# Row sums of the second block's mixer from a 65th column of the values that holds 1.0

## The reference, cut to what matters

```python
def hybrid_mixer(n, pos, ...):
    proj = n @ w_in          # c_q 256, c_kv 128, k_r 32, dq, dk, dv 384 each, mq, mk, mv 256 each
    o_a = mla_causal_attention(q_a, k_a, v_a)            # 6 heads, keys 64 + 32, values 64
    o_b = diff_causal_attention(q1, q2, k1, k2, dv, ...) # 6 heads, p = softmax(s1) - lam * softmax(s2)
    o_b = rmsnorm(o_b, sub_norm) * (1.0 - lam_init)
    o_c = moba_causal_attention(mq, mk, mv, ...)         # 4 heads of 64; at 256 tokens one block
    return concatenate([o_a, o_b, o_c]) @ w_out
```

## Time and profile before

| what | value |
|---|---|
| runs | 2402.16, 2405.36, 2407.83 us, median 2405.36 |
| profiled execution | 2401.76 us, its span 2400.0 us |
| TensorE, matmuls | 2357.4 us busy, 98% of the span |
| TensorE, weight loads | 1937.0 us, 81% |
| VectorE | 1726.6 us, 72% |
| ScalarE | 1446.9 us, 60% |
| GpSimd | 69.7 us, 3% |
| TensorE's granted clock | 0.998 of full speed |
| first layer's mixer of the second stack | attention from about 1575.6 to 1635 us |
| the same of the second layer | about 2009.4 to 2069 us |

### The profile page before, as it was taken

One profiled execution on the slowest core, in us unless ns is written; L12 is line 12 of the kernel. 1 busy time (PEld: TensorE's weight loads), 2 busy tenths in 40 slices (PEclk: granted clock), 3 DMA queues, 4 the chain that ended last, 5 costly groups with the idle time before them and its releaser, 6 DMA issues.

```text
span 2400.0 us, 32057 instructions
## 1 busy us (share of the span) xinstructions
PE 2357.4 (98%) x12122; PEld 1937.0 (81%) x12122; DVE 1726.6 (72%) x2111; ACT 1446.9 (60%) x1761; POOL 69.7 (3%) x79
## 2 busy tenths in 40 slices
PE   9999999999999999999999999999999999999998
PEld 8688888678888888888888888888888888887887
DVE  8664446769898988888989898766465565755555
ACT  6544444657777777777777777564544446554443
POOL 1000000001000000000000000001000000000000
PEclk9999999999999999999999999999999999999999
DMA  7545554429999999999999999516435542452651
GB/s 264 163 158 193 185 186 157 145 82 340 368 345 372 344 377 345 374 339 375 348 369 346 369 350 366 192 54 227 159 124 192 177 145 83 175 187 95 196 190 44
DMA packets 249706, 569.99 MB, mean 237 GB/s; under 512 B 9665, under 2 KB 20353, under 8 KB 249601
## 3 DMA queue, kind: packets, MB, share of 16 engines
q1 hardware_dynamic: 249456, 568.30, 67.1%
q10 hardware_dynamic: 144, 0.26, 0.0%
HBM read 562.82 MB, written 1.05 MB: 235 GB/s over the span
## 4 chain that ended last, share of the span: by engine, by line
PE 92%; DVE 5%; ACT 2%; issue 1%; POOL 0%; POOLq 0%; ACTq 0%; DVEq 0%
PE PS L911 26%; PE PS L913 26%; PE PS L912 26%; PE PS L1064 2%; PE PS L1119 1%; PE PS L1534 1%; PE PS L1076 1%; PE PS L1363 1%; PE PS L1183 1%; PE PS L983 1%; ACT SM L1806 1%; DVE Wl L2216 1%; PE PS L1008 1%; PE PS L1102 1%; PE PS L1324 1%
## 5 line engine op out<-in xcount | busy, mean ns | idle before, releaser
L2645 DVE TENSOR_TENSOR Wl<-ring,Wh 128x2048 fp32r<-128x2048 f32 x334 | 761.6, 2297 | 101.0 <-ACT Wh L1952 101.0
L1952 ACT ACTIVATE Wh<-ring 128x2048 fp32r<-128x2048 f32 x334 | 639.8, 1918 | 127.7 <-PE PS L913 127.7
L2216 DVE TENSOR_TENSOR Wl<-ring,Wh 128x2048 fp32r<-128x2048 f32 (+2 forms) x192 | 431.0, 2251 | 276.6 <-ACT Wh L1713 276.1
L1713 ACT ACTIVATE Wh<-ring 128x2048 fp32r<-128x2048 f32 (+2 forms) x192 | 361.6, 1890 | 235.2 <-PE PS L913 234.2
L911 PE MATMUL PS<-Wh,HTh 128*128 128x512 f32 (+3 forms) x1184 | 464.2, 392 | 4.7 <-DVE Wl L2216 2.4
L913 PE MATMUL PS<-Wh,HTl 128*128 128x512 f32 (+3 forms) x1184 | 456.4, 386 | 0.0
L912 PE MATMUL PS<-Wl,HTh 128*128 128x512 f32 (+3 forms) x1184 | 455.4, 385 | 0.0
L911 PE MATMUL PS<-Wh,xgh 128*128 128x512 f32 x896 | 354.3, 395 | 1.8 <-DVE Wl L2645 1.2
L913 PE MATMUL PS<-Wh,xgl 128*128 128x512 f32 x896 | 349.5, 390 | 0.0
L912 PE MATMUL PS<-Wl,xgh 128*128 128x512 f32 x896 | 348.9, 389 | 0.0
L911 PEld LDWEIGHTS PS<-Wh,HTh 128*128 128x128 f32 x1184 | 222.8, 188 | 50.4 <-issue 4.3
(11 more groups left out here) (349 smaller groups left out, 2422.4 us busy)
## 6 DMA issues: line engine op xcount, KB each, us to landing
ring<-in_moe_w_gate SPq DMA_DIRECT2D x112, 1024.0 KB, 6.9
ring<-in_moe_w_up SPq DMA_DIRECT2D x112, 1024.0 KB, 7.0
ring<-in_moe_w_down SPq DMA_DIRECT2D x112, 1024.0 KB, 6.8
ring<-in_mlp_w SPq DMA_DIRECT2D x64, 1024.0 KB, 5.2
ring<-in_w_in SPq DMA_DIRECT2D x27, 1024.0 KB, 5.3
ring<-in_w_out SPq DMA_DIRECT2D x16, 1024.0 KB, 7.1
ring<-in_cross_wkv SPq DMA_DIRECT2D x16, 1024.0 KB, 12.4
ring<-in_ffn_w_gate SPq DMA_DIRECT2D x14, 1024.0 KB, 5.1
```

What stands on the lines that cost most here:

```text
L1713: act.activation(Wh[:, i % SPLITS, 0:n], ring[:, r % RING, 0:n], ACT.Copy).then_inc(w_hi, 1)
L1952: act.activation(Wh[:, (base + i) % SPLITS, :], ring[:, (raw + i) % RING, :], ACT.Copy).then_inc(e_hi, 1)
L2216: dve.tensor_tensor(Wl[:, i % SPLITS, 0:n], ring[:, r % RING, 0:n], Wh[:, i % SPLITS, 0:n].bitcast(F32), ALU.subtract).then_inc(w_lo, 1)
L2645: dve.tensor_tensor(Wl[:, (base + i) % SPLITS, :], ring[:, (raw + i) % RING, :], Wh[:, (base + i) % SPLITS, :].bitcast(F32), ALU.subtract) ...
```

## The change

The value tiles of diff (`DVS`), moba (`MVS`) and MLA (`VV`) get 65 columns per head. VectorE writes 1.0 into the last of them, six small memsets a layer. The value products read 65 columns per head, so that the output has the row's sum behind its 64 numbers, and `end` takes the reciprocal from there, in PSUM. The exponentials lose the accumulator output, and the wait for the output four units back that protected `sums`. To lay the values out with gaps, `take_block` (blocks 2 and 3) and `take_last` use two copies where there was one. The columns of `proj` behind the diff values move: moba's q starts at 1574 (before: 1568), its k at 1830, its v at 2086. `proj` has 2352 columns instead of 2336 for each of two tiles, 128 bytes more. Cross attention and the first stack stay as they are.

```diff
--- before.py
+++ after.py
@@ -96,6 +96,12 @@
 C1W = 28 + CC * TAPS
 C2 = dict(attn=0, cross=8, mem=16, mlp=24, qn=32, kvn=34)
 C2W = 35
+VW = 65
+DV_AT = DV0
+MQ_AT = DV_AT + DIFF_H * VW
+MK_AT = MQ_AT + 256
+MV_AT = MK_AT + 256
+W2 = -(-(MV_AT + MOBA_H * VW) // 16) * 16
 B1W = 4 * HD
 B2W = HD + 4 * DIFF_D
 
@@ -128,7 +134,7 @@
         HTh = sb("HTh", [P, KC, S], F32R)
         HTl = sb("HTl", [P, KC, S], F32R)
         proj_at = nc.sbuf_base
-        proj = sb("proj", [P, T, IN2])
+        proj = sb("proj", [P, T, W2])
         scr_at = nc.sbuf_base
         scr = sb("scr", [P, 6656])
 
@@ -202,7 +208,9 @@
         CQT = QT[:, 12:15, :]
         KN = H[:, :, 0:MLA_H * NOPE].rearrange("p t (h d) -> p t h d", d=NOPE)
         QN = proj[:, :, 0:MLA_H * NOPE].rearrange("p t (h d) -> p t h d", d=NOPE)
-        VV = scr[:, 22 * S:25 * S].rearrange("p (t h d) -> p t h d", t=T, h=MLA_H)
+        VV = scr[:, 22 * S:22 * S + T * MLA_H * VW].rearrange("p (t h d) -> p t h d", t=T, h=MLA_H)
+        DVS = proj[:, :, DV_AT:DV_AT + DIFF_H * VW].rearrange("p t (h d) -> p t h d", d=VW)
+        MVS = proj[:, :, MV_AT:MV_AT + MOBA_H * VW].rearrange("p t (h d) -> p t h d", d=VW)
         QR = scr[:, 18 * S:21 * S].rearrange("p (t h d) -> p t h d", t=T, h=2 * MLA_H)
         KR4 = H[:, :, 768:896].rearrange("p t (n d) -> p t n d", n=4)
         MEM = scr[:, 0:T * D].rearrange("p (t d) -> p t d", t=T)
@@ -361,7 +369,8 @@
 
             n = len(scores)
             apart = 2 if n == 2 and dv < P else 1
-            return dict(t=t, kl=kl, one=one, scores=scores, bias=bias, scale=scale, values=values, dv=dv, end=end, dst=dst,
+            wide = VW if one and end[0] != "nsa" else dv
+            return dict(t=t, kl=kl, one=one, wide=wide, summed=wide > dv, scores=scores, bias=bias, scale=scale, values=values, dv=dv, end=end, dst=dst,
                         kbs=kbs or [P] * (kl // P), needs=needs, slots=slice(0, n * apart, apart))
 
         def o_bank(un, u):
@@ -441,7 +450,7 @@
                         for h in (ha, hb):
                             r, slot = (64 * (h % 2) + k * DIFF_D, h // 2) if h < 4 else (k * DIFF_D, h - 2)
                             sc.append([(QT[r:r + DIFF_D, slot, tok(t)], QT[r:r + DIFF_D, 4 + slot, 0:kl])])
-                            val.append([proj[:, kb, DV0 + h * 64:DV0 + h * 64 + 64] for kb in range(t + 1)])
+                            val.append([DVS[:, kb, h, :] for kb in range(t + 1)])
                             slopes.append(-SLOPES[h] / scale)
                     dst = heads_of(H[:, t, 384:768], DIFF_H)[:, ha:hb + 1:hb - ha, :]
                     out_.append(unit(t, kl, sc, ("slopes", dist[:, t, 0:kl], slopes), scale, val, 64, ("diff", layer), dst))
@@ -456,7 +465,7 @@
                 for h in order:
                     r = 64 * (h % 2)
                     sc.append([(QT[r:r + 64, 8 + h // 2, tok(t)], QT[r:r + 64, 10 + h // 2, 0:kl])])
-                    val.append([proj[:, kb, MV0 + h * 64:MV0 + h * 64 + 64] for kb in range(t + 1)])
+                    val.append([MVS[:, kb, h, :] for kb in range(t + 1)])
                 scale = 64 ** -0.5
                 bias = ("slopes", dist[:, t, 0:kl], [-SLOPES[DIFF_H + h] / scale for h in order])
                 dst = H[:, t, 768:1024].rearrange("p (b a d) -> p a b d", a=2, b=2)
@@ -522,7 +531,7 @@
             t_diff.append(chunks_batch([plain_chunk(proj, c0), plain_chunk(proj, c0 + P)], slot))
             t_diff.append(chunks_batch([plain_chunk(proj, c0 + 256, 64), plain_chunk(proj, c0 + 320, 64)], slot + 2, 64))
         t_moba = [chunks_batch([plain_chunk(proj, c0 + P * b) for b in range(2)], slot)
-                  for c0, slot in ((MQ0, 8), (MK0, 10))]
+                  for c0, slot in ((MQ_AT, 8), (MK_AT, 10))]
         qn, kn = ([plain_chunk(src, P * b) for b in range(3)] for src in (proj, H))
         qr = [plain_chunk(QR.rearrange("p t h d -> p t (h d)"), P * b) for b in range(3)]
         kr = [plain_chunk(H, 768)]
@@ -1113,10 +1122,10 @@
                         pe.wait_ge(o_out, u)
                     elif u >= 2:
                         pe.wait_ge(o_out, u - 1)
-                    dv = un["dv"]
+                    wide = un["wide"]
                     for m, vs in enumerate(un["values"]):
                         for kb, v in enumerate(vs):
-                            mm = pe.matmul(PS[:, o_bank(un, u), m * dv:(m + 1) * dv],
+                            mm = pe.matmul(PS[:, o_bank(un, u), m * wide:(m + 1) * wide],
                                            PT[0:un["kbs"][kb], u % 2, kb, m, :], v,
                                            start=(kb == 0), stop=(kb == len(vs) - 1))
                     mm.then_inc(o_full, 1)
@@ -1799,10 +1808,13 @@
                 def exps(i):
                     u, un = u0 + i, units[i]
                     act.wait_ge(sm_ready, u + 1)
-                    if u >= 4:
+                    if u >= 4 and not un["summed"]:
                         act.wait_ge(o_out, u - 3)
                     for m in range(len(un["scores"])):
                         row = SM[:, u % 2, m, 0:un["kl"]]
+                        if un["summed"]:
+                            ins = act.activation(row, row, ACT.Exp, bias=nb[:, u % 2, m:m + 1], scale=un["scale"])
+                            continue
                         ins = act.activation(row, row, ACT.Exp, bias=nb[:, u % 2, m:m + 1], scale=un["scale"],
                                              accum_out=sums[:, u % 4, m:m + 1])
                     ins.then_inc(p_ready, 1)
@@ -2093,18 +2105,36 @@
                     ahead()
                     norm(col2(layer, "attn", 8), BY_HALF)
 
+                def spread_heads(dst, src, rs_t):
+
+                    return act.activation(dst, src.rearrange("p (h d) -> p h d", d=64), ACT.Copy, scale=rs_t)
+
                 def take_block(k):
                     c0, n = IN2_BLOCKS[k]
                     for t in range(T):
-                        take(proj[:, t, c0:c0 + n], scale=row_rs[:, 0, t:t + 1])
+                        rs_t = row_rs[:, 0, t:t + 1]
+                        if k < 2:
+                            take(proj[:, t, c0:c0 + n], scale=rs_t)
+                            continue
+                        c.lin += 1
+                        act.wait_ge(lin_full, c.lin)
+                        src = PS[:, 4 + (c.lin - 1) % 4, :]
+                        if k == 2:
+                            spread_heads(DVS[:, t, 0:4, 0:64], src[:, 256:512], rs_t)
+                            act.activation(proj[:, t, c0:c0 + 256], src[:, 0:256], ACT.Copy, scale=rs_t).then_inc(lin_out, 1)
+                        else:
+                            spread_heads(DVS[:, t, 4:6, 0:64], src[:, 0:128], rs_t)
+                            act.activation(proj[:, t, MQ_AT:MQ_AT + 384], src[:, 128:512], ACT.Copy,
+                                           scale=rs_t).then_inc(lin_out, 1)
 
                 def take_last(t):
 
                     c0, n = IN2_BLOCKS[4]
                     c.lin += 1
                     act.wait_ge(lin_full, c.lin)
-                    act.activation(proj[:, t, c0:c0 + n], PS[:, 6, 0:n], ACT.Copy,
-                                   scale=row_rs[:, 0, t:t + 1]).then_inc(lin_out, 1)
+                    rs_t = row_rs[:, 0, t:t + 1]
+                    act.activation(proj[:, t, MK_AT + 128:MK_AT + 256], PS[:, 6, 0:128], ACT.Copy, scale=rs_t)
+                    spread_heads(MVS[:, t, :, 0:64], PS[:, 6, 128:384], rs_t).then_inc(lin_out, 1)
 
                 def take_heads(parts, width):
 
@@ -2136,7 +2166,7 @@
                         take_heads((QN, QR), NOPE + MROPE)
                         turn(t_diff)
                     elif k == 3:
-                        take_heads((KN, VV), NOPE + MLA_V)
+                        take_heads((KN, VV[:, :, :, 0:MLA_V]), NOPE + MLA_V)
                 attention(diff_units(layer) + moba_units() + mla_units(), mix_extras,
                           {0: another, 4: another}, {2: lambda: take_last(0), 4: lambda: take_last(1)})
                 turn_mix(t_mixed)
@@ -2397,8 +2427,9 @@
                     n, dv, t, dst, kind = len(un["scores"]), un["dv"], un["t"], un["dst"], un["end"]
                     dve.wait_ge(o_full, u + 1)
                     cf = coef[:, u % 2, 0:n]
-                    seq(dve.reciprocal(cf, sums[:, u % 4, 0:n]))
-                    o = heads_of(PS[:, o_bank(un, u), 0:n * dv], n)
+                    o = heads_of(PS[:, o_bank(un, u), 0:n * un["wide"]], n)
+                    seq(dve.reciprocal(cf, o[:, :, dv] if un["summed"] else sums[:, u % 4, 0:n]))
+                    o = o[:, :, 0:dv]
                     tmp = otmp[:].rearrange("p (m d) -> p m d", m=4)
                     if kind[0] == "plain":
                         by = bc4(cf, dv)
@@ -3014,6 +3045,9 @@
                 c.piece += 2
                 ahead()
                 dve.wait_ge(lin_out, base + 2)
+                for values_ in (DVS, MVS, VV):
```

(2 more changed lines are left out.)

## The result

| kernel | median | profiled execution, its span |
|---|---|---|
| before (the three runs above and a fourth) | 2406.24 us (2402.16 to 2407.83, 4 runs) | 2401.76, 2400.0 |
| after | 2433.02 us (2429.84 to 2437.95, 4 runs) | 2429.84, 2428.1 |

The ratio is 1.0104, 95% interval 1.0085 to 1.0123. The forecast was 2403.5 us and "no difference"; the range ended at 2407.5.

The account below looks back on a forecast made before the run. TensorE, busy for 98% of the span, was taken as the bound; two idle gaps closing gave 0.41 + 0.52 = 0.93 us a layer, 1.9 us in all, from median 2405.36 to 2403.5 us; range 2399.5 to 2407.5.

Parts of the forecast that it names:

- The tile's 128 bytes move addresses only, at no cost: Projection tile grown by 128 bytes: claimed to shift only the addresses of what follows, cost nothing.
- The slower rival: Value products (L1119, 264 records) stream or write 65 columns slowly; at a quarter rate +29.6 us, 2433 us; chance 0.04.
- The rule of lines of two fp32 numbers in PSUM: Value outputs of heads 1 and 3 start inside a PSUM line; by this rule the sum would become the slower case.
- Gap A: TensorE idle before the transposes at 1586.41, waiting for exponentials of units 0 and 1; claimed to close, 0.41 us a layer.
- gap E: TensorE idle before 1606.42, waiting for exponentials of units 4 and 5; claimed to close, 0.52 us a layer.
- An exponential saves 0.10 us: ScalarE in the mixers: each of 88 exponentials drops its accumulator read, 0.10 us each, 8.8 us of ScalarE in all.
- Split takes: Copies of projection blocks in two instructions: +0.16 us on the late block's path; others 0.15 to 0.16 us each, covered.
- Memsets: VectorE, six a layer ahead of the latents' sums of squares: 0.4 us, covered, cost nothing; 0.8 us in both layers if uncovered.
- Reciprocal out of PSUM: VectorE reads the row sums in PSUM: claimed to cost nothing, with 0.1 us a layer as the other end.
- The moved q and k of the block attention: Stationary side of 8 transposes a layer, now starting at column 1574: taken as nothing, between 0 and 0.9 us a layer.
- the bound of 1.8 us: Most that the shifted stationary operand of the block attention's transposes was allowed to cost, kept for the range.
- Every other stage as long as before: Sign to look for: mixer of a layer 0.9 us shorter, all other stages unchanged in length.

Follow-up runs that it names:

- gap kernels: Unused bytes between projection and scratch tiles: kernel before with 128 bytes 2436.42 us, 64 bytes 2441.26 us, 32 bytes 2436.93 us; changed kernel with 128 bytes 2404.91 us.
- the changed kernel with the gap: Changed kernel plus 128 unused bytes between the projection tile and the scratch tile: 2404.91 us against 2407.69 us of before, ratio 0.9985.

## Why the prediction was wrong, step by step

- **The step that failed** is the sentence "The tile's 128 bytes move addresses only, at no cost; no row bounds it better". It moved the stationary tiles of 5136 products out of step with the moving weights, and each lost 5 to 6 ns: 27 us. It had no term in the sum, no bound and no rival, although it is the one edit that reaches every stage. Only the kernel before with 128 unused bytes, 28.7 us slower, showed the term.
- The slower rival stood at 2433 us, the measured time, with another cause. That was chance: the value products with 65 columns keep their step. In the chain of waits of the changed kernel a unit's 16 records take

```profile
1638.09 1.73 PE PS L1128 x16
```

  as in the earlier trace rows, and the mixer got shorter. The rule of lines of two fp32 numbers in PSUM (the Trainium skill, Advanced Engine Details and Errata, Memory Cachelines) shows no cost in this layout, in which the run of each head is contiguous: the records keep the floor of 0.108 us. A cost that stays under that floor could not be seen here.
- Gap A and gap E: right. Forecast 0.41 and 0.52 us; in the first mixer TensorE came 0.44 and 0.47 us earlier there. The mixers gained 1.07 and 1.31 us where the forecast had 0.93 each, and the rest lies at small waits that it had no term for. 0.11 us more was gained between the fillers ahead of unit 4's transposes and the value products behind them. And the second layer has not quite the same shape: there the transposes of unit 0 waited for the exponentials as well, 0.46 us from the last projection product to them where 0.17 are enough, and that wait is gone too (0.29 us). First before, then the changed kernel:

```profile
2015.47 0.34 PE L913 MATMUL PS<-Wh,HTl 128*128 128x384 f32 x1
2015.93 0.63 PE L1076 MATMUL PS<-ident,SM 128*128 128x128 f32 x4
...
2043.03 0.34 PE L922 MATMUL PS<-Wh,HTl 128*128 128x384 f32 x1
2043.20 0.60 PE L1085 MATMUL PS<-ident,SM 128*128 128x128 f32 x4
```

- An exponential saves 0.10 us: right, to 0.01 us. From the first of unit 1's four (256 columns) to the copy behind them are 1.97 us before (1583.71 to 1585.68) and 1.60 after (1609.93 to 1611.53), 0.09 us each. With unit 0's four (128 columns) it is 1.54 before and 1.18 after, 0.09 us each.
- Split takes: the 128-column part takes 364 to 367 ns (forecast 372), the 256-column part 467 to 479 (476); the second starts 0.25 us after the first. Both together take 0.73 us where one took 0.58: +0.15 us, and +0.16 was forecast. Where the exponentials stay slow, TensorE waits for it at the transposes of unit 4, as the run with the accumulators kept shows.
- Memsets: 62 to 63 ns each, with no wait of TensorE behind them. They overlap each other and the sums of squares behind them:

```profile
1564.88 0.09 DVE L3050 MEMSET proj<- 128x6 f32 x3
1564.91 0.42 DVE L3055 CUSTOM_DVE_ANT_0 SM<-proj 128x256 f32<-128x256 f32 x1
```

- Reciprocal out of PSUM: 180 ns for 4 numbers against 176 out of SBUF; right at nothing.
- The moved q and k of the block attention: transposes at 276 ns a record, as before (277); the bound of 1.8 us wasn't needed.
- "Every other stage as long as before" was named as the sign to look for. It is the one that broke, and it led to the cause.

The clock adds a part of its own: around 496 to 512 us the changed kernel's execution was granted 0.68 and before's 0.89, and 480 to 496 us 0.89 and 1.00, together 5 us more of missing clock. Up to the first mixer the slow records take 23.7 us more from start to start (4368 of them), where 26.6 us were lost; with the clock's 5 that would be 28.8, 2 us more than was lost, which I leave open. In the two stretches behind it the records give 2.1 and 2.2 us, and 2.05 and 1.85 were lost. With the gap kernels the same places vary from run to run. Whether the shift has any hand in the clock is open.

## What to carry to other kernels

A change of one tile's size moves every tile behind it. If a kernel streams long products, note the distance of each stationary tile to its moving tile, and try it at a multiple of 256 bytes, which was the fast place in all runs here; two groups of the same instruction that differ by a few ns a record, split by tile, are the sign. To judge an edit that resizes a tile, time the old kernel with only the padding beside it: that one run separates placement from the edit. And where fillers stand behind a wait, a faster engine may pay in full only once they are cut (here some 0.4 us more a mixer).

## What the runs showed of the hardware that was not expected

- The pace of long rows of 512-column fp32r products depends on where the two operands lie to each other: 389 ns against 394 to 395 ns a record, 0.227 against 0.233 us from start to start. With 384 columns the difference is 1 to 2 ns. The fp32 products of this kernel show none (value products 271 ns with 64 or 65 columns and 379 with 256, products of 384 columns with the ring as the moving operand 499, in the kernel before and in the changed one). The Trainium skill, TensorE: Matmul & The Clock Gate (Step-by-step: what each phase is for), says that the engine has "two independent read ports", one for the moving operand and one for the loads of the stationary. The runs do not agree with full independence: only the distance of the two was changed, and the pace changed. By which part of the memory or the engine they meet was not tried, nor distances other than 0, 32, 64 and 128 bytes off a multiple of 256 (the multiples tried were 65536 bytes and 100608 bytes, and 100864 in the changed kernel with the gap).
- Single executions of the kernel before lie up to 12.5 us apart (2401.53 to 2414.06), and the granted clock goes with it: all those granted 0.998 took 2401.5 to 2402.5 us, all those granted 0.993 took 2412.1 to 2414.1. In the one execution taken apart (moved tiles behind the scratch) 11 us of span went with 12 us of missing clock, in two short places from 112 and from 496 us on.
